# Seven block products in place of eight for 12 of the 22 gate and up tiles of three feed-forward blocks, with weight sums on GpSimd

## The reference, cut to what matters

```python
def _swiglu(h, w_gate, w_up, w_down):
    return (jax.nn.silu(h @ w_gate) * (h @ w_up)) @ w_down

for layer in range(DEPTH):                     # DEPTH = 2
    ...                                        # attention
    h = h + _swiglu(_rmsnorm(h, norm_ffn[layer]), w_gate[layer], w_up[layer], w_down[layer])
...
u = rmsnorm(h, norm2_w[l]) * (1.0 + sc2) + sh2  # third layer: modulated norm
ff = (jax.nn.silu(u @ w_ffn_gate[l]) * (u @ w_ffn_up[l])) @ w_ffn_down[l]
```

## Time and profile before

| | |
|---|---|
| median of 3 runs | 1936.92 us (1936.15 to 1940.04) |
| profiled execution, first to last instruction | 1933.8 us |
| PE busy | 1894.7 us (98%) |
| weight loads of PE busy | 1539.7 us (80%) |
| DVE busy | 1098.2 us (57%) |
| ACT busy | 909.3 us (47%) |
| POOL busy | 136.0 us (7%) |
| mean granted TensorE clock | 0.992 of full speed |

### The profile page before, as it was taken

One profiled execution on the slowest core, in us unless ns is written; L12 is line 12 of the kernel. 1 busy time (PEld: TensorE's weight loads), 2 busy tenths in 40 slices (PEclk: granted clock), 3 DMA queues, 4 the chain that ended last, 5 costly groups with the idle time before them and its releaser, 6 DMA issues.

```text
span 1933.8 us, 25245 instructions
## 1 busy us (share of the span) xinstructions
PE 1894.7 (98%) x8980; PEld 1539.7 (80%) x8980; DVE 1098.2 (57%) x1666; ACT 909.3 (47%) x1517; POOL 136.0 (7%) x131
## 2 busy tenths in 40 slices
PE   7999999999999999999999999999999999999997
PEld 6778778888888777778888888878888788888886
DVE  5566555444466767655444446688767774444322
ACT  5556543232376544444444357765555442332322
POOL 0000020000011100001000002210111100000000
PEclk9999999999999999999999999999999999999999
DMA  3111123323366322223233345532221223222331
GB/s 139 66 65 65 44 76 109 102 93 98 104 212 200 122 88 87 87 74 100 92 103 94 102 134 188 192 102 68 70 73 64 66 87 100 96 98 95 91 100 63
DMA packets 56480, 193.68 MB, mean 100 GB/s; under 512 B 7136, under 2 KB 7648, under 8 KB 56416
## 3 DMA queue, kind: packets, MB, share of 16 engines
q1 hardware_dynamic: 47616, 163.47, 26.1%
q0 software_dynamic: 7696, 27.79, 4.5%
q10 hardware_dynamic: 1104, 1.58, 0.2%
HBM read 186.52 MB, written 2.10 MB: 98 GB/s over the span
## 4 chain that ended last, share of the span: by engine, by line
PE 90%; DVE 4%; ACT 3%; issue 1%; DMA 1%; SPq 0%; ACTq 0%; DVEq 0%
PE ps L373 26%; PE ps L375 26%; PE ps L374 26%; PE ps L2283 1%; PE ps L2148 1%; PE ps L1104 1%; PE ps L2129 1%; PE ps L2164 1%; PE ps L1129 1%; PE ps L1119 1%; DVE wlo L355 1%; PE ps L2152 1%; ACT whi L344 1%; PE ps L2331 0%; PE ps L2318 0%
## 5 line engine op out<-in xcount | busy, mean ns | idle before, releaser
L373 PE MATMUL ps<-xh,whi 128*128 128x512 f32 x1536 | 607.1, 395 | 5.1 <-DVE wlo L355 2.1
L375 PE MATMUL ps<-xh,wlo 128*128 128x512 f32 x1536 | 600.1, 391 | 0.0
L374 PE MATMUL ps<-xl,whi 128*128 128x512 f32 x1536 | 600.0, 391 | 0.0
L355 DVE TENSOR_TENSOR wlo<-raw,whi 128x1024 fp32r<-128x1024 f32 (+1 forms) x296 | 370.0, 1257 | 188.6 <-ACT whi L344 182.1
L344 ACT ACTIVATE whi<-raw 128x1024 fp32r<-128x1024 f32 (+1 forms) x304 | 311.6, 1034 | 160.6 <-PE ps L375 160.3
L373 PEld LDWEIGHTS ps<-xh,whi 128*128 128x128 f32 x1536 | 290.0, 189 | 68.9 <-issue 4.7
L375 PEld LDWEIGHTS ps<-xh,wlo 128*128 128x128 f32 x1536 | 289.6, 189 | 61.2
L374 PEld LDWEIGHTS ps<-xl,whi 128*128 128x128 f32 x1536 | 289.8, 189 | 60.7 <-issue 1.9
L373 PE MATMUL ps<-acth,whi 128*128 128x512 f32 x528 | 210.5, 399 | 0.0
L374 PE MATMUL ps<-actl,whi 128*128 128x512 f32 x528 | 205.9, 390 | 0.0
L375 PE MATMUL ps<-acth,wlo 128*128 128x512 f32 x528 | 205.6, 389 | 0.0
(11 more groups left out here) (327 smaller groups left out, 2257.5 us busy)
## 6 DMA issues: line engine op xcount, KB each, us to landing
raw<-in_gu SPq DMA_DIRECT2D x132, 512.0 KB, 3.3
raw<-in_down SPq DMA_DIRECT2D x48, 512.0 KB, 3.7
raw<-in_qkv SPq DMA_DIRECT2D x24, 512.0 KB, 4.2
wada<-in_ada POOLq DMA_DIRECT2D x24, 512.0 KB, 3.9
tmps<-in_ada POOLq DMA_DIRECT2D x24, 512.0 KB, 3.6
raw<-in_qkvb SPq DMA_DIRECT2D x24, 512.0 KB, 3.6
raw<-in_down SPq DMA_DIRECT2D x24, 384.0 KB, 3.1
raw<-in_recur SPq DMA_DIRECT2D x16, 512.0 KB, 3.4
```

The costliest lines, as they stand in the source:

```text
L355: eng.tensor_tensor(wlo[:, s, 0:n], raw[:, s, 0:n], whi[:, s, 0:n].bitcast(F32), ALU.subtract).then_inc(lo_done, 1)
L373: pe.matmul(ps[:, bank], whi[:, s, w], hi[:, k0 + k], start=start and k == 0, stop=False)
L374: pe.matmul(ps[:, bank], whi[:, s, w], lo[:, k0 + k], start=False, stop=False)
L375: mm = pe.matmul(ps[:, bank], wlo[:, s, w], hi[:, k0 + k], start=False, stop=stop and k == n - 1)
```

## The change

FAST = 6 groups of the stage, of two feature tiles each, are taken out of the loop; PLAIN = 5 iterations of the old form stay (the first one ahead of the new part, four behind it). Every group is two steps p: gate (even p) and up (odd p), 12 in a stage. A step treats two units as one 2x2 block product: weights in four blocks (input features 0 to 511 and 512 to 1023 by two output tiles), activations in four blocks (the same feature halves by tokens 0 to 255 and 256 to 511). It forms seven products in place of eight, each of 4 slices x 3 matmuls of 256 columns.

For this the activations' differences (`token_raw`, four sets, once a stage) and the weights' sums (`sums_first`, `sums_last`, four tensor_tensor of 512 columns a step) are formed on GpSimd. ACT and DVE split all of them into high and low parts. A copy of the normalised activations in float32 (`whole`) is made first by ACT. The partial results are taken out of PSUM by three ACT copies (`snap`) and the DVE steps `inner`, `last` and `outer`; gu0 and gu1 (scaled) multiply two of them by `rstd` in an instruction of its own. Weight groups are called "direct" (one raw unit), "first" and "last" (a pair of sums each) and "corner" (half a unit). Not printed below: `split_count` and `mm_count` (semaphore counts), `fast_group` (the slot and columns of a weight group), `fast_token_hi` and `fast_token_lo` (the same split for one token set of 1024 columns) and `fast_whole` (eight ACT copies of 512 columns, with scale). Semaphores of the attention stages are used again, `var` moves in memory, and the tiles' numbers in the loop shift.

```diff
+HALF = S // 2
+FAST = 6
+FAST_PAIRS = 2 * FAST
+PLAIN = FT // 2 - FAST
...
+        def fast_tiles(p):
+            i = p // 2
+            if p % 2:
+                return tmp[2], tmp[3]
+            return tmp[0], tmp[1] if i % 2 else sqsum
+        def fast_banks(p):
+            return (4, 5, 6) if p % 2 else (0, 1, 2)
+        def consumed(sp, x, p):
+            wait(sp, x.lo, split_count("corner", p))
+            wait(sp, x.sum, 4 * p + 4)
+        def fast_load(sp, u, x):
+            for p in range(FAST_PAIRS):
+                if p < 2:
+                    wait(sp, lo_done, u.number(0, 2 * p + 1) + 1)
+                else:
+                    consumed(sp, x, p - 2)
+                for n in range(2):
+                    tile = 2 + 2 * (p // 2) + n
+                    sp.dma_start(raw[:, 2 * (p % 2) + n, :], u.weights[2 * tile + p % 2, :, :]).then_inc(x.landed[p % 2].sem, 16)
...
+        def fast_pool_tokens(pool, x):
+            wait(pool, x.whole, 4)
+            first, second = whole[:, 0:4], whole[:, 4:8]
+            part = [token_raw[:, n].rearrange("p (k w) -> p k w", w=HALF) for n in range(4)]
+            pool.tensor_tensor(part[0], first[:, :, HALF:S], first[:, :, 0:HALF], ALU.subtract).then_inc(x.token.sem, 1)
+            wait(pool, x.whole, 8)
+            wait(pool, x.token, 1)
+            pool.tensor_tensor(part[1], second[:, :, HALF:S], part[0], ALU.subtract).then_inc(x.token.sem, 1)
+            fast_pool_first(pool, x, 0)
+            pool.tensor_tensor(part[2], second[:, :, HALF:S], first[:, :, HALF:S], ALU.subtract).then_inc(x.token.sem, 1)
+            wait(pool, x.token, 2)
+            pool.tensor_tensor(part[3], second[:, :, 0:HALF], part[1], ALU.subtract).then_inc(x.token.sem, 1)
+        def fast_pool_first(pool, x, p):
+            a11, a21, a22 = raw[:, 2 * (p % 2), 0:S], raw[:, 2 * (p % 2) + 1, 0:S], raw[:, 2 * (p % 2) + 1, S:2 * S]
+            fast_landed(pool, x, p)
+            if p:
+                wait(pool, x.lo, split_count("first", p - 1))
+            pool.tensor_tensor(sums_first[:, 0:S], a21, a22, ALU.add).then_inc(x.sum.sem, 1)
+            wait(pool, x.sum, 4 * p + 1)
+            pool.tensor_tensor(sums_first[:, S:2 * S], sums_first[:, 0:S], a11, ALU.subtract).then_inc(x.sum.sem, 1)
+        def fast_pool_last(pool, x, p):
+            a11, a12, a21 = raw[:, 2 * (p % 2), 0:S], raw[:, 2 * (p % 2), S:2 * S], raw[:, 2 * (p % 2) + 1, 0:S]
+            if p:
+                wait(pool, x.lo, split_count("last", p - 1))
+            else:
+                wait(pool, x.r.rstd, 4)
+            wait(pool, x.sum, 4 * p + 2)
+            pool.tensor_tensor(sums_last[:, 0:S], a12, sums_first[:, S:2 * S], ALU.subtract).then_inc(x.sum.sem, 1)
+            pool.tensor_tensor(sums_last[:, S:2 * S], a11, a21, ALU.subtract).then_inc(x.sum.sem, 1)
+        def fast_pool(pool, x):
+            fast_pool_tokens(pool, x)
+            fast_pool_last(pool, x, 0)
+            for p in range(1, FAST_PAIRS):
+                fast_pool_first(pool, x, p)
+                fast_pool_last(pool, x, p)
...
+        def fast_hi(act, x, group, p):
+            if group in ("direct", "corner"):
+                fast_landed(act, x, p)
+            else:
+                wait(act, x.sum, 4 * p + (2 if group == "first" else 4))
+            if group == "corner" and p >= 2:
+                wait(act, x.mm, mm_count(4, p - 2))
+            elif group != "corner" and p:
+                wait(act, x.mm, mm_count({"direct": 2, "first": 6, "last": 7}[group], p - 1))
+            source, s, w = fast_group(group, p)
+            act.activation(whi[:, s, w], source, ACT.Copy).then_inc(x.hi.sem, 1)
+        def fast_lo(dve, x, group, p):
+            wait(dve, x.hi, split_count(group, p))
+            source, s, w = fast_group(group, p)
+            dve.tensor_tensor(wlo[:, s, w], source, whi[:, s, w].bitcast(F32), ALU.subtract).then_inc(x.lo.sem, 1)
...
+                i, final = p // 2, p == FAST_PAIRS - 1
+                first, second = fast_tiles(p)
+                bank_a, bank_b, bank_c = fast_banks(p)
+                if p == 0:
+                    wait(act, mm_done, u.number(0, 3) + 1)
+                    fast_hi(act, x, "corner", 0)
+                fast_hi(act, x, "last", p)
+                wait(act, x.mm, mm_count(1, p))
+                if p % 2:
+                    wait(act, f.lo, 2 * i + 1)
+                elif i:
+                    wait(act, x.prod, 2 * i - 1)
+                else:
+                    wait(act, f.prod, 1)
+                act.activation(first[:, 0:HALF], ps[:, bank_a, 0:HALF], ACT.Copy).then_inc(x.snap.sem, 1)
+                if p % 2:
+                    silu(i, 0)
+                    if i:
+                        hidden_hi(i - 1, 1)
+                elif i:
+                    hidden_hi(i - 1, 0)
+                if final:
+                    wait(act, x.mm, mm_count(2, p))
+                    split_hi(act, u, (1, 0))
+                else:
+                    fast_hi(act, x, "direct", p + 1)
+                wait(act, x.mm, mm_count(5, p))
+                if p % 2:
+                    wait(act, f.lo, 2 * i + 2)
+                elif i >= 2:
+                    wait(act, x.prod, 2 * i - 2)
+                elif i == 1:
+                    wait(act, f.prod, 2)
+                act.activation(second[:, HALF:S], ps[:, bank_c, 0:HALF], ACT.Copy).then_inc(x.snap.sem, 1)
+                if not final:
+                    fast_hi(act, x, "corner", p + 1)
+                wait(act, x.mm, mm_count(6, p))
+                act.activation(first[:, HALF:S], ps[:, bank_a, 0:HALF], ACT.Copy).then_inc(x.snap.sem, 1)
+                if final:
+                    split_hi(act, u, (1, 1))
+                else:
+                    fast_hi(act, x, "first", p + 1)
+                if p % 2:
+                    silu(i, 1)
...
+            def inner(p):
+                second = fast_tiles(p)[1]
+                wait(dve, x.mm, mm_count(7, p))
+                wait(dve, x.snap, 3 * p + 2)
+                dve.tensor_tensor(second[:, HALF:S], ps[:, fast_banks(p)[0], 0:HALF], second[:, HALF:S], ALU.add)\
+                   .then_inc(x.inner.sem, 1)
+                if x.scaled:
+                    wait(dve, x.inner, 2 * p + 1)
+                    dve.tensor_tensor(second[:, HALF:S], second[:, HALF:S], rstd[:, HALF:S], ALU.mult).then_inc(x.inner.sem, 1)
+            def last(p):
+                second = fast_tiles(p)[1]
+                wait(dve, x.mm, mm_count(4, p))
+                if x.scaled:
+                    dve.tensor_tensor(second[:, 0:HALF], ps[:, fast_banks(p)[0], 0:HALF], rstd[:, 0:HALF], ALU.mult)\
+                       .then_inc(x.last.sem, 1)
+                else:
+                    dve.tensor_copy(second[:, 0:HALF], ps[:, fast_banks(p)[0], 0:HALF]).then_inc(x.last.sem, 1)
+            def outer(p):
+                first, bank = fast_tiles(p)[0], fast_banks(p)[1]
+                wait(dve, x.mm, mm_count(3, p))
+                wait(dve, x.snap, 3 * p + 3)
+                both = first[:, :].rearrange("p (a w) -> p a w", w=HALF)
+                dve.tensor_tensor(both, ps[:, bank:bank + 2, 0:HALF], both, ALU.add).then_inc(x.outer.sem, 1)
+                if x.scaled:
+                    wait(dve, x.outer, 2 * p + 1)
+                    dve.tensor_tensor(first[:, :], first[:, :], rstd[:, :], ALU.mult).then_inc(x.outer.sem, 1)
+            def hidden(i, second):
+                gate, up = fast_tiles(2 * i)[second], tmp[2 + second]
+                wait(dve, x.silu, 2 * i + second + 1)
+                if second:
+                    wait(dve, x.last, 2 * i + 2)
+                    wait(dve, x.inner, x.steps * (2 * i + 2))
+                else:
+                    wait(dve, x.outer, x.steps * (2 * i + 2))
+                dve.tensor_tensor(up[:, :], gate[:, :], up[:, :], ALU.mult).then_inc(x.prod.sem, 1)
+            def hidden_lo(i, second):
+                m = 2 + 2 * i + second
+                wait(dve, f.hi, m + 1)
+                dve.tensor_tensor(actl[:, m], tmp[2 + second][:, :], acth[:, m].bitcast(F32), ALU.subtract).then_inc(f.lo.sem, 1)
+            for p in range(FAST_PAIRS):
+                i, final = p // 2, p == FAST_PAIRS - 1
+                if p:
+                    inner(p - 1)
+                if p == 0:
+                    fast_lo(dve, x, "corner", 0)
+                fast_lo(dve, x, "last", p)
+                if final:
+                    split_lo(dve, u, (1, 0))
+                else:
+                    fast_lo(dve, x, "direct", p + 1)
+                if i:
+                    hidden_lo(i - 1, p % 2)
+                if not final:
+                    fast_lo(dve, x, "corner", p + 1)
+                if p:
+                    last(p - 1)
+                if p % 2 == 0 and i:
+                    hidden(i - 1, 1)
+                if final:
+                    split_lo(dve, u, (1, 1))
+                else:
```

(149 more changed lines are left out.)

221 lines of the change are left out of this document (138 added, 83 removed).

## The result

The changed kernel takes 1992.57 us (median, 1992.2 to 1998.56) against 1937.19 us of the kernel before, run beside it: ratio 1.0296, 95% interval 1.0283 to 1.0309. The forecast was 1994 us with a range of 1936 to 2035.

The account below looks back on a forecast made before the run. PE bounded the old kernel; the new steps were to be bound by DVE and POOL taking turns. Steps, starts and ends summed to +22.0 us each in gu0 and gu1 and +13.3 in gu2, together +57: 1994 us, range 1936 to 2035.

Parts of the forecast that it names:

- PE's step, 9.91 us: PE in each new step: 84 matmuls of 256 columns at 0.118 us, 0.97 us less than before.
- DVE's own part, 7.77 us: DVE's operations and waits in a gu0 or gu1 step, without POOL's effect: 7.77 us; in gu2 6.54.
- Taking turns, 1.16 us a sum: POOL's sums block DVE's SBUF work: four a step add 4.64 us, except where DVE reads PSUM or waits.
- The step, 11.3 and 10.3 us: Length of a new step, set by DVE and POOL together: 11.3 us in gu0 and gu1, 10.3 in gu2.
- a copy of ACT waits for `hidden_lo` and comes a little late: Odd steps: allowance for this late ACT copy, raising the step from 11.2 to 11.3 us.
- The start, 14.2 + 1.4 us in gu0: Step 0 of gu0: 14.2 us lost to DVE's and POOL's queues, 1.4 to a lower clock; gu2 16.5 with 1.4.
- hidden but for POOL's lock: Stage start: the `whole` copies delay the fourth unit's high part on ACT, claimed to cost nothing beyond POOL's lock.
- The end, 2.8 us and 1.4 for the block: Step 11: the fourth product waits 2.8 us for `inner` behind `outer` and `hidden` on DVE, plus 1.4 for the block.
- Sum: All three stages: +22.0 us each in gu0 and gu1, +13.3 in gu2, together +57.
- POOL costs DVE nothing: Rival for steps and starts: PE's 9.91 us rules, starts lose 4.8, 4.4 us less a stage, 1924 us; chance 0.18.
- Both cancel: Rival: steps of about 10.4 us and starts of 8 to 10 us, giving 1933 to 1941 us; chance 0.08.
- The pace by weight loads: Rival on PE: 256-column matmuls at 0.17 us for weight loads, steps of 14.3 us, 2060 us and over; chance 0.02.

Follow-up runs that it names:

- experiment 1: Changed kernel with every GpSimd sum replaced by constant fills in 64-column pieces, same waits and signals: 1930.42 us, ratio 0.9962.
- experiment 4: Changed kernel with only DVE's order altered, `hidden_lo` ahead of the split of "direct", sums still on POOL: 1985.03 us, ratio 1.0251.
- experiment 9: Kernel of experiment 8 with "first" sums also on DVE (POOL idle) and gu2's later token high parts behind ACT's second copy: 1933.38 us, ratio 0.9982.
- experiment 2: Changed kernel with only the four token sums at each stage's start replaced by constant fills, weight sums kept: 1978.88 us, ratio 1.022.
- experiment 3: Changed kernel with all sums moved to DVE, right ahead of the splits of "direct" and "first", POOL idle in the stages: 1973.42 us, ratio 1.0194.
- experiment 5: Changed kernel with FAST = 3, six new steps a stage in place of twelve, eight plain iterations in place of five: 1982.78 us, ratio 1.0236.
- experiment 6: Changed kernel in experiment 4's order, POOL keeping only the two "first" sums, DVE making "last" and token sums: 1964.66 us, ratio 1.0141.
- experiment 7: Kernel of experiment 6 with `whole` ahead of the norm's root, token sums around the norm, second evacuation before the last token splits: 1951.94 us, ratio 1.0074.
- experiment 8: Kernel of experiment 7 with gu2's third and fourth token splits behind ACT's first copy, POOL's first sums behind the modulation: 1949.7 us, ratio 1.0062.

## Why the prediction was right

**PE's step, 9.91 us**: 10.08. The price of a matmul was 0.120 us, not 0.118; the upper bound. That would be 2 us a stage too good, but it counts only where PE rules: in the changed kernel steps 1, 10 and 11 of gu0 (10.26 and twice 10.08 us) and of gu1, and the even steps of gu2.

**DVE's own part, 7.77 us**: 7.76 in experiment 1.

**Taking turns, 1.16 us a sum**: held; L726 and L727 end 1.12 and 1.14 us after DVE's end, and the 3.41 us that four sums were to add to a step are some 3.4 (experiments 1 and 4). The Trainium skill (SBUF — State Buffer, SBUF: two separate sides) has the pair of ports locked for the whole instruction; that is right to about 0.15 us of the 1.29 here.

**The step, 11.3 and 10.3 us**: mis-sized by 0.35 and 0.2. The means over steps 1 to 10 are 11.65 and 10.49, and step 11, with no raw sums behind it, is 10.08. The forecast saw "a copy of ACT waits for `hidden_lo` and comes a little late" and gave it 0.1; experiment 4 prices it at 0.3 (0.24 in gu2). With it the wait of PE stood elsewhere than forecast: `last` holds a step's first block for 0.5 us at most, and the 2.3 us of the odd steps are ahead of the sixth block. One step of 14.23 us, in part at the lower clock, in each of gu0 and gu1 is 1.5 us over the other odd ones, of which the step behind it gives 0.6 back (10.08 for 10.67); the forecast had neither. Eleven steps: 126.6 us in gu0 for 124.3.

**The start, 14.2 + 1.4 us in gu0**: step 0 was to end at 324.5 and ended at 325.8 (323.1 less 309.0 is 14.1; the 14.2 is a slip of no weight). Its parts were off: PE's first iteration ended 3.8 us late, not 1.1, since the fourth unit's high part was late on ACT as well ("hidden but for POOL's lock" it wasn't), and the rest lost 13.0. In gu1 the first iteration came only 0.6 us late, so the start lost 13.5 there. In gu2 it lost 15.0 + 0.6 where 16.5 + 1.4 stood.

**The end, 2.8 us and 1.4 for the block**: the wait was 1.8, in gu2 0.7; the block 1.5. 1 to 2 us a stage too much.

**Sum**: `down` starts 24.8 us late behind gu0 (22.0 forecast), 21.1 more behind gu1 (22.0), 10.7 more behind gu2 (13.3): 56.6 in all where 57 stood. That the total is nearer than its terms is luck: steps were put too short by about 2 us a stage and gu0's start by 1, ends too long by 1 to 2, and the starts of gu1 and gu2 too long by 2.

**The rivals.** "POOL costs DVE nothing" is what experiment 1 builds: 1930 us. Faster, as that rival says, but not its 1924, since a step is 10.08 us and not 9.91, and the starts lose 5.6 us in the mean for its 4.8. "Both cancel" didn't come in this kernel; experiment 9 lands in its range of times, with its steps (10.31) but with starts of 3 us in gu0 and gu1 where it has 8 to 10. The pace by weight loads did not occur.

What stays open: how much of the starts' loss in gu2 can be removed (8.1 us in experiment 9, with DVE busy 16.46 of 16.60 us), and whether the lower clock in step 9 comes from the waits in the odd steps. The runs speak for it without proving it: experiments 2, 3 and 5, whose odd steps wait for the same copy, also have stretches of 3.4 us at the lower clock among their steady steps (from 398.0 in gu0 of experiment 2, from 353.1 in experiment 3, from 991.0 in gu1 of experiment 5), and experiments 1, 4 and 6 to 9 have none past a stage's first two steps.

## What to carry to other kernels

A saving of 7% on the busiest engine counts only in steps that this engine still bounds, and the fixed costs come first: here 29 us of matmuls saved, and 21 us of starts and ends even with no sums to make (experiment 1). GpSimd isn't free help for a kernel whose VectorE works from SBUF: a sum of 1.29 us there takes 1.16 us from VectorE, which does the same sum in 0.61 itself; give such sums to GpSimd only where VectorE reads PSUM or waits. Here even the two sums a step that were meant to fall there cost 5 us a stage (experiment 9). When one engine becomes full, look next for copies that wait for the tile that it still has to read: the order of one instruction was worth 0.3 us a step with the sums on POOL, and the rearranged start 8.0 and 6.6 us in gu0 and gu1, but nothing in gu2 (experiment 7).
